# Compressed branches of a sparse-attention block: the first-layer products of keys and values issued in turn into two column groups, with their weights fetched half by half

## The reference, cut to what matters

```
def _compress(raw, pos, w1, w2):
    kk = raw.reshape(b_, nh, CMP_STRIDE, N_KV, HEAD_DIM)
    blocks = jnp.concatenate([kk[:, i:i + nc] for i in range(n_sub)], axis=2)
    blocks = blocks + pos[None, None, :, None, :]
    flat = blocks.transpose(0, 1, 3, 2, 4).reshape(b_, nc, N_KV, CMP_LEN * HEAD_DIM)
    return jax.nn.gelu(flat @ w1) @ w2

k_cmp = _compress(kc_raw, cmp_pos, ck_w1, ck_w2)
v_cmp = _compress(vc_raw, cmp_pos, cv_w1, cv_w2)
```

## Time and profile before

| | us |
|---|---|
| median of 3 runs | 3490.41 |
| lowest, highest | 3489.88, 3494.08 |
| the profiled execution, device time | 3487.15 |
| its span | 3485.4 |

### The profile page before, as it was taken

How to read it: one execution, slowest core, us unless ns; L and a number is a source line. 1 busy time by engine, 2 the same in 40 slices (tenths; PEclk the granted TensorE clock), 3 DMA queues, 4 the chain that set the end, 5 groups by cost and what they waited for, 6 DMA issues and landing times.

```text
span 3485.4 us, 45135 instructions
## 1 busy us (share of the span) xinstructions
PE 3381.8 (97%) x18422; PEld 2838.7 (81%) x18422; DVE 2016.8 (58%) x2039; ACT 1535.3 (44%) x1561; POOL 321.3 (9%) x364
## 2 busy tenths in 40 slices
PE   6999899999999999999999999999999999999998
PEld 4875678888888888888888899999888788888886
DVE  2655567775566554444444579896555544444445
ACT  3423356653455443433333455663443434333343
POOL 1000000000000000000000137662000000000000
PEclk9999999999999999999999999999999999999999
DMA  9999667776766665656556656667435556555553
GB/s 350 355 349 348 180 209 227 221 224 225 194 185 186 198 199 192 193 186 196 189 191 192 176 157 159 184 187 236 152 112 191 172 190 193 185 194 190 191 191 135
DMA packets 529863, 713.21 MB, mean 205 GB/s; under 512 B 12951, under 2 KB 347103, under 8 KB 524192
## 3 DMA queue, kind: packets, MB, share of 16 engines
q1 hardware_dynamic: 509888, 647.01, 58.9%
q0 software_dynamic: 15024, 59.53, 5.1%
q10 hardware_dynamic: 4784, 4.27, 0.4%
HBM read 702.09 MB, written 11.82 MB: 205 GB/s over the span
## 4 chain that ended last, share of the span: by engine, by line
PE 82%; DVE 8%; ACT 4%; issue 2%; DMA 2%; POOL 1%; ACTq 0%; SPq 0%; DVEq 0%; POOLq 0%
PE ps L2796 9%; PE ps L2798 9%; PE ps L2797 9%; PE ps L2654 8%; PE ps L2655 8%; PE ps L2658 8%; PE ps L2584 7%; PE ps L2585 3%; DVE w_lo L1522 3%; ACT w_hi L927 2%; DMA stage<-in_w_ada 2%; PE ps L2603 2%; PE ps L2604 1%; PE ps L2605 1%; PE ps L2618 1%
## 5 line engine op out<-in xcount | busy, mean ns | idle before, releaser
L1522 DVE TENSOR_TENSOR w_lo<-stage,w_hi 128x2048 fp32r<-128x2048 f32 x480 | 1108.4, 2309 | 1092.1 <-ACT w_hi L927 1080.5
L927 ACT ACTIVATE w_hi<-stage 128x2048 fp32r<-128x2048 f32 x476 | 911.4, 1915 | 1300.5 <-PE ps L2798 561.7
L2796 PE MATMUL ps<-w_hi,xt 128*128 128x512 f32 x1408 | 550.9, 391 | 3.8 <-DVE xt L1584 2.3
L2798 PE MATMUL ps<-w_hi,xt 128*128 128x512 f32 x1408 | 548.6, 390 | 0.0
L2797 PE MATMUL ps<-w_lo,xt 128*128 128x512 f32 x1408 | 548.4, 389 | 0.0
L2584 PE MATMUL ps<-xt,w_hi 128*128 128x512 f32 x1320 | 471.6, 399 | 6.2 <-DVE w_lo L1522 5.5
L2654 PE MATMUL ps<-w_hi,hid_hi 128*128 128x512 f32 x1152 | 449.6, 390 | 5.9 <-DVE w_lo L1522 5.9
L2655 PE MATMUL ps<-w_lo,hid_hi 128*128 128x512 f32 x1152 | 448.3, 389 | 0.0
L2585 PE MATMUL ps<-xt,w_lo 128*128 128x256 f32 x1320 | 370.6, 281 | 0.0
L2658 PE MATMUL ps<-w_hi,hid_lo 128*128 128x512 f32 x1152 | 354.8, 389 | 0.0
L2796 PEld LDWEIGHTS ps<-w_hi,xt 128*128 128x128 f32 x1408 | 264.7, 188 | 58.9 <-DVE xt L1584 2.5
(11 more groups left out here) (447 smaller groups left out, 4501.6 us busy)
## 6 DMA issues: line engine op xcount, KB each, us to landing
stage<-in_w_in SPq DMA_DIRECT2D x88, 1024.0 KB, 5.7
stage<-in_w_up SPq DMA_DIRECT2D x88, 1024.0 KB, 5.8
stage<-in_ffn_w_gate SPq DMA_DIRECT2D x88, 1024.0 KB, 5.2
stage<-in_ffn_w_up SPq DMA_DIRECT2D x88, 1024.0 KB, 5.2
stage<-in_ffn_w_down SPq DMA_DIRECT2D x88, 1024.0 KB, 5.5
stage<-in_w_ada SPq DMA_DIRECT2D x64, 1024.0 KB, 7.9
stage<-in_w_down SPq DMA_DIRECT2D x44, 1024.0 KB, 5.7
stage<-in_w_out SPq DMA_DIRECT2D x32, 1024.0 KB, 5.6
```

The lines of the kernel that those rows point to most:

```text
L927: act.activation(w_hi[:, u % 2 * UNIT:(u % 2 + 1) * UNIT], slot(u % SLOTS), ACT.Copy).then_inc(hi_made, 1)
L1522: dve.tensor_tensor(w_lo[:, part], slot(u % SLOTS), w_hi[:, part].bitcast(F32), ALU.subtract).then_inc(split_made, 1)
L2796: pe.matmul(dst, chunk(xt_hi, k, m), wh, start=k == 0, stop=False)
L2798: last = pe.matmul(dst, chunk(xt_lo, k, m), wh, start=False, stop=k == KC - 1)
```

## The change

PE now runs `compress(u)` over halves instead of over keys and values: the first call does the first eight steps of both, the second call the last eight of both, and within a call keys and values alternate. The key product goes to partitions 0 to 59 of bank 4, the value product to partitions 64 to 123 of bank 5, which are two column groups of the array. The first half of the key weights goes to slot 0 and the first half of the value weights to slot 1; the second halves follow when `direct_used` reaches 1. It now counts to 2. The first call needs `raw_k` and `raw_v` both, so DVE makes half of `raw_k` before the last projection split. Both `hidden` calls stand after `glu_tanh(0)` on ACT, both `turn_hidden` calls after `glu(2)` on PE.

```diff
--- before.py
+++ after.py
@@ -517,22 +517,21 @@
             return slot(s).rearrange("p (k n) -> p k n", n=T)
 
         mix_split = plan["mix"][1]
-        for x, w in enumerate(("cmp_k_w1_2", "cmp_v_w1_2")):
-            view = I[w].rearrange("(h k p) n -> h p k n", p=P, k=8)
-            for u in range(2):
-                if x == 0:
-                    sp.wait_ge(split_made, mix_split - SLOTS + 1 + u)
+        for u in range(2):
+            for x, w in enumerate(("cmp_k_w1_2", "cmp_v_w1_2")):
+                if u == 0:
+                    sp.wait_ge(split_made, mix_split - SLOTS + 1 + x)
                 else:
-                    sp.wait_ge(direct_used, u + 1)
-                sp.dma_start(slot_pair(u), view[u]).then_inc(landed[u], 16)
-            for g in (2 * x, 2 * x + 1):
+                    sp.wait_ge(direct_used, 1)
+                sp.dma_start(slot_pair(x), I[w].rearrange("(h k p) n -> h p k n", p=P, k=8)[u]).then_inc(landed[x], 16)
+            for g in (2 * u, 2 * u + 1):
                 at = mix_place(g)
                 sp.wait_ge(split_made, mix_split + g - 1)
                 sp.dma_start(slot_pair(at % SLOTS), column_pair(I[("ssm_glu_w1_2", "ssm_glu_w2_2")[g % 2]], g // 2)).then_inc(landed[at % SLOTS], 16)
         for g in range(4, 16):
             at = mix_place(g)
             if g < 6:
-                sp.wait_ge(direct_used, g - 1)
+                sp.wait_ge(direct_used, 2)
             else:
                 sp.wait_ge(split_made, mix_split + g - 3)
             sp.dma_start(slot_pair(at % SLOTS), column_pair(I[("ssm_glu_w1_2", "ssm_glu_w2_2")[g % 2]], g // 2)).then_inc(landed[at % SLOTS], 16)
@@ -844,6 +843,10 @@
     NUM = (0, 1, 6, 7)
     TILE_BANK = (0, 1, 6)
     CMP_BANK = (4, 2, 5, 3)
+
+    def hidden_bank(x):
+
+        return ps[64 * x:64 * x + 60, (4 + x) * 512:(4 + x) * 512 + T]
 
     def scores_of(m):
 
@@ -1434,17 +1437,17 @@
             act.activation(glu_x[:, p % 2 * 512:(p % 2 + 1) * 512], bank(7), ACT.Tanh, scale=0.5).then_inc(S["glu_e"], 1)
 
         def hidden(x):
-            act.wait_ge(direct_used, 2 * x + 2)
+            act.wait_ge(direct_used, 2)
             if x == 0:
                 for s in range(4):
                     act.wait_ge(sg_sent[s], 16 * 8)
-            act.activation(hid_n[:, x * T:(x + 1) * T], bank(4 + x, 0, T, 60),
+            act.activation(hid_n[:, x * T:(x + 1) * T], hidden_bank(x),
                            ACT.Gelu_apprx_tanh).then_inc(S["hn_gelu"], 1)
 
-        hidden(0)
         split_glu(2)
         split_glu(3)
         glu_tanh(0)
+        hidden(0)
         hidden(1)
         split_glu(4)
         split_glu(5)
@@ -2306,10 +2309,10 @@
             dve.tensor_copy(swp[0:64, br * 512:(br + 1) * 512], src[64:128, :])
             dve.tensor_copy(swp[64:128, br * 512:(br + 1) * 512], src[0:64, :]).then_inc(S["swapped"], 1)
 
-        def blocks(x):
+        def blocks(x, groups):
 
             raw = (raw_k, raw_v)[x]
-            for g in range(NKV):
+            for g in groups:
                 src = pt2[g % 2 * 64:g % 2 * 64 + 64, (16 + 2 * x + g // 2) * T:(17 + 2 * x + g // 2) * T]
                 tok = src.rearrange("p (i l two) -> p two l i", l=8, two=2)
                 pos = pos_t[g % 2 * 64:g % 2 * 64 + 64, :].rearrange("p (l two) -> p two l", two=2)
@@ -2319,7 +2322,8 @@
                         last = dve.tensor_tensor(
                             dst[:, 8 * lh:8 * lh + 8, 15 * g:15 * g + 15], tok[:, two, :, lh:lh + 15],
                             pos[:, two, 8 * lh:8 * lh + 8].unsqueeze(2).to_broadcast([64, 8, 15]), ALU.add)
-            last.then_inc(S["raw_made"], 1)
+            if g == NKV - 1:
+                last.then_inc(S["raw_made"], 1)
 
         for t in range(60):
             if t == 0:
@@ -2340,6 +2344,8 @@
             elif 4 <= t < 28:
                 split("in2", 0, 0, t - 4)
             elif t >= 28:
+                if t == 59:
+                    blocks(0, range(2))
                 split("gg", 0, 0, t - 28)
             if t == 0:
                 continue
@@ -2379,9 +2385,9 @@
                         make_c(s // 2)
                     elif s >= 3:
                         rest_y((s - 3) // 2)
-        blocks(0)
+        blocks(0, range(2, 4))
         sum_y(7)
-        blocks(1)
+        blocks(1, range(4))
         rest_y(7)
 
         def glu_first(p):
@@ -2415,10 +2421,10 @@
         glu_first(0)
         split_glu(2)
         split_glu(3)
-        turned_hidden(0)
         link.then(dve.memset(hid_v[:, :], 0.0))
         glu_rest(0)
         glu_first(1)
+        turned_hidden(0)
         turned_hidden(1)
         split_glu(4)
         dve.wait_ge(S["kv_made"], 1)
@@ -3171,19 +3177,20 @@
 
         mix = plan["mix"][1]
 
-        def compress(x):
-
-            pe.wait_ge(S["raw_made"], x + 1)
-            pe.wait_ge(*((S["cw_made"], 8) if x else (S["bt_copied"], 16)))
-            raw = (raw_k, raw_v)[x]
-            for u in range(2):
-                pe.wait_ge(landed[u], 16 * (plan["mix"][0] // SLOTS + x + 1))
-                for k in range(8):
-                    kk = 8 * u + k
-                    last = pe.matmul(bank(4 + x, 0, T, 60), raw[:, kk * 60:(kk + 1) * 60],
-                                     stage[:, u * UNIT + k * T:u * UNIT + (k + 1) * T],
+        def compress(u):
+
+            if u == 0:
+                pe.wait_ge(S["raw_made"], 2)
+                pe.wait_ge(S["bt_copied"], 16)
+                pe.wait_ge(S["cw_made"], 8)
+            for x in range(2):
+                pe.wait_ge(landed[x], 16 * (plan["mix"][0] // SLOTS + u + 1))
+            for kk in range(8 * u, 8 * u + 8):
+                for x in range(2):
+                    last = pe.matmul(hidden_bank(x), (raw_k, raw_v)[x][:, kk * 60:(kk + 1) * 60],
+                                     stage[:, x * UNIT + kk % 8 * T:x * UNIT + (kk % 8 + 1) * T],
                                      start=kk == 0, stop=kk == 15)
-                last.then_inc(direct_used, 1)
+            last.then_inc(direct_used, 1)
 
         def glu_tile(g, tile):
 
@@ -3211,8 +3218,8 @@
         glu(0)
         glu(1)
         compress(1)
+        glu(2)
         turn_hidden(0)
-        glu(2)
         turn_hidden(1)
         glu(3)
         pe.wait_ge(S["ht_copied"], 2)
```

## The result

The changed kernel takes 3497.68 us (median of 22 runs, 3493.70 to 3503.13). The kernel before, run beside it, takes 3493.18 (22 runs, 3489.88 to 3498.38). The ratio is 1.0016 with a 95% interval of 1.0010 to 1.0022: slower by 5.6 us, between 3.5 and 7.7 (the two medians differ by 4.5). The forecast was 3493.5 us, +3.1 on a base of 3490.41, with a range up to 3497.5; the measured median lies 0.2 us above that range. The direction was right, the sum too small.

The account below looks back on a forecast made before the run. PE was taken as the bound, by 2.4 to 3.6 us, with the weight stream behind it. Products -6.84, wait +8.4, clock +1.7 and transposes 0.26 gave +3.6, taken as +3.1 on 3490.41: 3493.5 us, range 3487.0 to 3497.5.

Parts of the forecast that it names:

- Part 1: Compress products on PE: alternating column groups cut each call from 7.05 to 3.63 us, -6.84 us together.
- Part 2: Before compress(0): the first call now needs raw_v too; no wait taken, at most 0.3 us.
- Part 3: Weight DMA queue: second halves land about 2415.4, just in time for compress(1), wanted at 2415.57.
- Part 4: Before glu(2): POOL's 1.5 MB burst, now earlier, holds up g2; 8.4 us of new wait, bounds 3.5 to 9.5.
- Part 5: Behind PE's wait before glu(2): granted clock falls to 0.50, costing +1.7 us, bounds 0 to 3.4.
- Sum of these: At glu(3): start at 2436.1 where it was 2432.50, +3.6 us; +3.1 taken.
- a burst up to 2 us sooner: Before compress(1): last value weights caught, PE stops there instead, clock recovers by glu(2); sum +1.9 us.
- A: At glu(2): burst doesn't catch g2; -1.5 us, or -3.2 without the clock; 3488 us; chance 0.22.
- B: At glu(2): g2 lands by 2414.9, full gain of -6.8 us, 3483.6 us; chance 0.04.
- C: Compress calls: 60-column groups don't run side by side, g2 lands near 2426; 3496.4 us; chance 0.10.
- Part 6: After glu(2): joined transposes add 0.26 us before glu(3); from there the shift is carried unchanged to the end.

Follow-up runs that it names:

- e8_order: Changed kernel with g2 fetched before the second weight halves, compress(1) between glu(2)'s tiles, POOL's 1.5 MB fetch issued once ACT copied g4; 3487.62 us, ratio 0.9986.
- e5_one_group: Changed kernel with the value product on partitions 0 to 59, so both products lie in one column group; 3495.18 us, ratio 1.0005.
- e3_late_burst: Changed kernel with POOL's second fetch into sg_a (1.5 MB) held back until ACT has copied g3; 3491.70 us, ratio 0.9998.
- e2_after: Changed kernel run once more, no edit; 3497.33 us, ratio 1.0010 to the kernel before.
- e4_keep_clock: Changed kernel with 34 unread products of 128 x 512 between compress(1) and glu(2) to keep PE busy; 3494.68 us, ratio 1.0004.
- e11_after_scores: Changed kernel with the 64 score products split into two runs of 32 around a tile of glu(5); 3495.67 us, ratio 1.0008.
- e10_before_shift: Kernel before with 5 unread products of 128 x 512 ahead of the second-layer products, a 1.1 us shift; 3495.88 us, ratio 1.0006.
- e7_late_clock: e3_late_burst plus 14 unread products of 128 x 512 before glu(2) to keep PE busy; 3491.39 us, ratio 0.9996.
- e9_before_late: Kernel before with only POOL's second fetch held back until ACT has copied g3; 3492.62 us, ratio 1.0002.

## Why the prediction was right, and where it was wrong

**Part 1, right.** 3.62 us (3.60 in e8_order) where 3.63 was worked out from the state read-out. e5_one_group shows the cause.

**Part 2, right.** compress(0) waited for nothing. raw_v was ready at 2402.86, 0.3 us before it, the cover that was worked out.

**Part 3, right.** The second halves landed 8.0 and 10.6 us after their issue, in time for compress(1), which started 15.3 us after compress(0), as forecast, directly behind glu(1). The stream was not quite the one of before, though. Before, its second half had been issued alone, at 2407.3, and q1 moved only 0.47 MB between 2408 and 2411; after, both halves were issued together, the first packets came after 2409, and from there q1 ran at 0.35 MB per us. The last value weights landed 14.6 us after the start of compress(0) where 15.2 was forecast.

**Part 4, right in that the burst catches g2, 0.9 us too dear, and resting on a misread row.** The wait was 7.85 us. The forecast's own stretch, from 2419.2 to 2427.9, is 8.7; its 8.4 leaves out the 0.26 us of transposes that no longer stand before glu(2). Of the 0.9, half is not the burst's: without a burst, in e3_late_burst, ACT takes g2 at 17.7, and the forecast had kept the 18.2 of before. The burst adds 4.7 where the forecast had 5.0.

The misread row is the earlier trace rows. It was taken for a burst that stops the weight stream almost wholly. What q1 had moved by 2419, before (from 2404.5) and after (from 2406; packets, MB, share of 16 engines):

```profile
q1 hardware_dynamic: 4076, 4.12, 88.0%
```
```profile
q1 hardware_dynamic: 3243, 3.27, 78.8%
```

The four fetches in the queue are 4 x 1024 KB, 4.19 MB. Before, 0.07 MB of them were left when the burst began, so the 0.06 MB of the earlier trace rows are what q1 still had, not what it was allowed. After, 0.9 MB were left, and q1 moved 0.07 MB per us beside the burst: 285 packets to 270 on q0, one for one. Four more traces have 0.5 to 1.0 MB left at that point (e2_after, e4_keep_clock, e5_one_group, e11_after_scores), and in each q1 has 271 to 273 packets in 4 us to 271 or 272 on q0. The Trainium skill, "DMA: Bandwidth & Descriptors", section "Queues, rings and completion order", says that an engine goes round its queues packet by packet. Where both queues had work these five traces agree, if the packets that the profile counts are those that the page means; so the 0.07 MB per us that the prediction worked out by that rule was right, and the earlier trace rows was no case against it. That the price still came near follows from the sum of bytes and not from the row: as long as g2 isn't through before the burst is, all 1.57 MB of the burst pass ahead of its end, an estimate of 1.57 / 0.35 = 4.5 us however the queues share. What stays open is why the last 0.02 MB of before took from 2420 to 2425.85.

**Part 5, right.** +1.7 forecast, 1.92 read, 2.0 by e4_keep_clock: a wait of 7.85 us, and the granted clock is 0.50 behind it. The rule cited there, of the Trainium skill, "TensorE: Matmul & The Clock Gate", section "Why this matters for your kernels", on idle gaps between bursts of matmuls, agrees with this stretch. The row that the size was taken from is less clear than it was read: at the earlier trace rows PE stood still for 1.39 us only, among products of 128 x 128 and 128 x 64, and whether the stop alone made that fall wasn't tried.

**Sum of these:** glu(3) at +3.6 by the sum of the parts, +3.1 as taken, measured +2.73. The 3.1 is nearer only because it was drawn towards a case that didn't come, a burst up to 2 us sooner. To here the forecast held, and rivals A, B and C are refuted for this kernel: ACT took g2 at 22.4 and not 18.2, PE did wait, and the calls did overlap. C's price was wrong as well: with slow products the rest of the change costs nothing in M (37.99).

**Part 6, the failed step:** "From glu(3) on all engines follow PE as before, so the shift is carried to the end." The engines did follow as before, but the shift was not carried, it grew: the tail, put at +0, is 2.8 and 4.2 us longer in the two profiles of the changed kernel. In both, 3.0 us come from a stretch at half clock at the 64 score products, where the records of PE leave no gap; later falls, shorter or longer than before, make the rest. e10_before_shift gets one by five products of 1.1 us alone, e11_after_scores takes it away. The prediction had looked for falls of the clock only where PE would stand still, and put no term on a shift. e7_late_clock, e8_order and e3_late_burst show that it is no matter of sign: with a gain in M the tail is longer too, by 1.6 to 3.0. With 3.0 in the sum the forecast would have been +6.1, where +5.6 (3.5 to 7.7) was measured, and +3.5 (0.3 to 6.6) in e2_after. Shown by taking it away is the fall itself, in the traces; in the timed runs its removal (1.0008 against 1.0016) stays within the uncertainty.

The rest of the miss is not in the kernel. The forecast stood on a median of three runs, 3490.41; all 22 put it at 3493.18, and thirty-three more in each set at 3492.2 to 3493.1. Of the 4.2 us between 3493.5 and 3497.68 this makes 2.8, and on the base of 3493.18 the same +3.1 would have given 3496.3.

**What stays open.** Why the kernel before has the score products where the clock does not fall, while in all kernels with another M (and the products undivided) it does, down to a difference of 0.13 us in e5_one_group. Whether the position, or what else those edits changed ahead of it, decides wasn't separated. Nor was it settled which of the later falls, near 2587 and 2744, is longer in an execution. In e2_after the first is 6.8 us, in the first profile of the changed kernel it is absent and the second is 6.8. The difference of 1.45 us between these two tails goes with such stretches; what decides them wasn't found.

## What to carry to other kernels

When an engine becomes faster, ask of each DMA issue that follows it what is in flight at the moment to which it moves: here a fetch that had come 0.5 us behind the weights came ahead of them, and cost more than half of the gain, and it took the order of fetches (e8_order), not faster products, to keep it. Compare kernels between landmarks in two traces, one at each end of the changed stretch and one at the end of the span, since a difference that arises behind the change is invisible in its own stretch. A queue that moves little beside another may be held up or may have little left: add up what it has moved against what was issued before reading its rate. And where the granted clock is part of the time, a gain or loss in one stretch may come with more from stretches at half clock further on (here 1.3 to 4.2 us with the score products undivided), so a forecast of this size needs a term, or at least a bound, for it.

## What the runs showed of the hardware that was not expected

- The granted clock fell to 0.50 with PE busy for all of 4.00 us, among or within 0.8 us behind 64 products of 64 x 15 that take 3.7 us at full clock, in eight profiles of seven kernels. In two runs of 32 with a tile of wide products between them, in three kernels with one profile each, there was no fall there. In the kernel before, undivided, there was none either. The records had no gap in any of them.
- At the score products such a stretch was 3.4 or 6.8 us long. From the second-layer products to the turns it took 23.36 us without a fall, 24.8 to 24.9 with 3.4 us of it and 26.4 with 6.8 us, so it cost 1.5 or 3.0.
- In the two profiles of the kernel before and the one of e9_before_late, M and tail agree within 0.05 us.
- Beside a burst on q0 of 4 KB packets, q1, with 1 KB packets and 0.5 MB or more left to move, got one packet for each of q0's and so 0.07 MB per us of the 0.35 that it had alone, in five traces.
